# Second pair's attention: where in its step VectorE divides a finished block of rows

## The chip, the cores and the metric

One core of a Trainium2 chip runs the whole program. The metric is device time in microseconds (us) of that core, as the median of separate executions. The profile is one further execution, seen by the hardware profiler.

Engines by the profile's short names: PE is TensorE (matrix products, and transposes as products with the identity), PEld its weight loads, DVE is VectorE, ACT is ScalarE, POOL is GpSimd, SP is SyncE.

## The reference, cut to what matters

Two blocks of two layers each. The change lies in the second block, in the attention part of each of its two layers ("the second pair"). All is float32, with 512 positions and 64 numbers per head. Each layer has three kinds of attention, side by side:

```
a:  6 heads, scores q.k + bias, restricted by a mask (dilated windows), softmax, times v
b:  4 heads, two softmaxes per head:  a = softmax(s1) - lam * softmax(s2);  o = a @ v
    o_b = rms_norm(o) * subln_g * (1 - lam_init)
c:  6 heads of width 96, causal softmax(q.k * scale) @ v
heads = concatenate(o_a, o_b, o_c);  h = layer_norm(ALPHA * x + heads @ w_o)
```

A softmax is kept as unnormalised exponentials until after the product with v. The block of 128 rows that comes out is then divided by its sums. That division is what the change moves.

## The kernel before, in words

The attention of a layer is cut into 80 *units*: one head, one softmax, one block of 128 query rows `i`, and 128, 256, 384 or 512 keys. A unit of kind b comes as two units next to each other (first and second softmax), all others are single. `UNITS` (line 705) is their order. Units 0 to 7 are done early, among projections. The rest go through a software pipeline of steps `st` = 8 to 83, and every engine's program is a loop over the same steps, written out by hand in this order:

- PE (lines 2352 to 2370): `score(st)`, the product q.k of unit `st` into one of three PSUM banks; then, when it is due, `mix(g)`, the products with v of a whole group `g` of finished units; then the transposes of unit `st - 4` (line 2367); then, at five steps, `turn_chunk` (line 2325), the transposes of finished heads.
- ACT (lines 1595 to 1616): copy the transposed unit out of PSUM (line 1602), then `exp2(st)` (lines 1563 and 1566).
- DVE (lines 3066 to 3088): `rows_out2` for a group whose mix is done, then `scored(st)` (line 2986: adds mask or bias to the score and takes the row minimum, from PSUM to SBUF), then `pair(st - 2)` if unit `st - 2` is the second of two (lines 2994 to 2996: joins the two softmaxes of a b unit), then `sub_norm` (two pieces of the norm of the b heads, steps 71 and 72), then the low part `g_lo` of a turned chunk (line 2530).
- POOL (line 942, `two_keys`): makes a head's keys in high and low parts when the last score of an earlier head is done (lines 944 and 947). Its program is no loop over steps.

What ties the engines together: `score(st)` on PE waits until DVE has done `scored(st - 3)`, whose bank it takes. `scored(st)` waits for `score(st)` and for a free SBUF buffer out of five. `exp2(st)` waits for `scored(st)`. `pair(i)` waits for `exp2(i)`, and PE's transposes of unit `i`, four steps after its score, wait for `exp2(i)` or, for a b unit, for `pair(i)`.

`rows_out2` is called with the rank of a turned unit and does something only for the last unit of a group. There are 13 groups: group 0 holds four b blocks; each later group holds the four row blocks of one a or c head, and up to two b blocks more, which are called *singles* in the code. For a group it issues a reciprocal for each single (line 3053), waits for `mix(g)`, takes the reciprocal of four sums (line 3056; for group 0 it is line 3050, ahead of the wait), multiplies 128x256 numbers (line 3057), and then one 128x64 multiply per single (line 3062). Its result is needed by `mix(g + 2)`, which takes the same PSUM bank, and by `turn_chunk`. It acts at these steps (worked out from lines 676 to 771):

```
group      0   1   2   3   4   5   6   7   8   9  10  11
step      15  23  29  37  43  51  57  63  70  74  78  82
singles    0   2   1   2   1   2   1   1   2   0   0   0
steps of the loop with a pair() behind scored(): 15 20 25 30 35 40 44 49 54 59 64
turn_chunk at steps 31 45 59 72 80 (and low part g_lo two steps later)
```

Group 12 is divided after the loop.

Of the kernel before, what the change touches and what calls it, by code (L numbers as in the profile page):

```python
# [262 lines left out]
def _program(nc, I, out, seen):  # L263
    ctx = ExitStack()
    with ctx:
# [444 lines left out]
        def probs_of(i):  # L710

            return strips[:, B_HEADS + EARLY_AT[i], :] if i < EARLY else sc2[(i - EARLY) % N_B]
# [5 lines left out]
        def turns(step):  # L718
            i = step - (N_B - 1)
            return UNITS[i]["rank"] if 0 <= i < len(UNITS) else None  # L720
# [132 lines left out]
        def _(sp):  # L853
            for half in range(2):
                t = 2 * half
                sp.dma_start(res[:, t:t + 2, :], I["x"][0, t * P:(t + 2) * P, :].rearrange("(t p) d -> p t d", p=P)).then_inc(s_x_landed[half].sem, 16)
            for n, (what, _) in enumerate(stream):
                if what == Q0:
                    sp.dma_start(raw_q0[:], I["tiles"][n, :, :]).then_inc(s_q0_landed.sem, 16)
# [1655 lines left out]
        def _(dve):  # L2515
            V = nc.vector

            def step(ins):

                ins.then_inc(s_dve_step.sem, s_dve_step.nth("latest"))  # L2520
                dve.wait_ge(s_dve_step.sem, s_dve_step.count)

            def inverse(key, a, n):

                dve.wait_ge(s_root.sem, s_root.at(key))
                step(V.reciprocal(rstd[:, a:a + n], rstd[:, a:a + n]))

            def lo_part(dst, src, hi, key, wait_key):
                dve.wait_ge(s_hi.sem, s_hi.at(wait_key))
                V.tensor_tensor(dst, src, hi.bitcast(F32), ALU.subtract).then_inc(s_lo.sem, s_lo.nth(key))  # L2530
# [407 lines left out]
            for l in range(DEPTH):  # L2938
# [42 lines left out]
                def scored(i):  # L2981

                    u = UNITS[i]
                    n = u["n"]
                    dve.wait_ge(s_scores.sem, s_scores.at((y, i)))
                    V.tensor_tensor_reduce(probs_of(i)[:, 0:n], ps[:, S_BANKS[i % N_S], 0:n], u["mask"], 1.0, 3.0e38, ALU.add, ALU.min,  # L2986
                                           small[:, 0, i % 8:i % 8 + 1]).then_inc(s_scored.sem, s_scored.nth((y, i)))

                def pair(i):

                    u = UNITS[i]
                    n, ratio = u["n"], small[:, 2, i % 8:i % 8 + 1]
                    dve.wait_ge(s_probs.sem, s_probs.at((y, i)))
                    step(V.reciprocal(ratio, small[:, 1, i % 8:i % 8 + 1]))
                    step(V.tensor_scalar(ratio, ratio, sums[:, u["sum"]:u["sum"] + 1], lam[:, 4:5], ALU.mult, ALU.mult))
                    V.scalar_tensor_tensor(probs_of(i)[:, 0:n], probs_of(i)[:, 0:n], ratio, probs_of(i - 1)[:, 0:n],
                                           ALU.mult, ALU.add).then_inc(s_paired.sem, s_paired.nth((y, i)))
# [21 lines left out]
                def sub_norm(st):  # L3019

                    o = ao[:, :, 384:640].rearrange("p t (h d) -> p t h d", d=HD)
                    sq = sq_b[:].rearrange("p (t h) d -> p t h d", t=XT)
                    if st == B_DONE + 1:
                        dve.wait_ge(s_o_out.sem, s_o_out.at((y, max(group_of[last_of["b", h]] for h in range(B_HEADS)))))
                        step(V.tensor_tensor(sq, o, o, ALU.mult))
                    if st == B_DONE + 2:
                        step(V.tensor_reduce(ssq[:, 0:16], sq_b[:], AX_X, ALU.add))
                        V.tensor_scalar(ssq[:, 0:16], ssq[:, 0:16], 1.0 / HD, 1e-5, ALU.mult, ALU.add).then_inc(s_var.sem, s_var.nth((y, "sub")))
                    if st == STEPS:
                        inverse((y, "sub"), 0, 16)  # L3030
                        step(V.tensor_scalar(rstd[:, 0:16], rstd[:, 0:16], lam_c[:, 1:2], None, ALU.mult))
                        r = rstd[:, 0:16].rearrange("p (t h) -> p t h", t=XT).unsqueeze(3).broadcast_to((P, XT, B_HEADS, HD))
                        step(V.tensor_tensor(o, o, r, ALU.mult))
                        g = subln[:].unsqueeze(1).unsqueeze(1).broadcast_to((P, XT, B_HEADS, HD))
                        V.tensor_tensor(o, o, g, ALU.mult).then_inc(s_sub.sem, s_sub.nth(y))

                def rows_out2(r):

                    g = group_of[r]
                    if r != GROUPS[g][-1]:  # L3040
                        return
                    b = OUT_BANKS[g % 2]
                    singles = [] if g == 0 else [q for q in GROUPS[g] if UNITS[RANKS[q]]["kind"] == "b"]
                    u = [UNITS[RANKS[q]] for q in GROUPS[g] if q not in singles][0]
                    w = HD if g == 0 else VW
                    rows = ps[:, b, 0:XT * w].rearrange("p (i d) -> p i d", d=w)
                    s0 = u["sum"] - u["i"]
                    totals = recips[:, s0:s0 + XT].unsqueeze(2)
                    if g == 0:
                        step(V.reciprocal(totals, sums[:, s0:s0 + XT].unsqueeze(2)))  # L3050
                    for q in singles:
                        x = UNITS[RANKS[q]]
                        V.reciprocal(recips[:, x["sum"]:x["sum"] + 1], sums[:, x["sum"]:x["sum"] + 1]).then_inc(s_b_recip.sem, s_b_recip.nth((y, q)))
                    dve.wait_ge(s_mixed.sem, s_mixed.at((y, g)))
                    if g > 0:
                        step(V.reciprocal(totals, rows[:, :, HD:VW]))
                    m = V.tensor_tensor(ao[:, :, u["col"]:u["col"] + HD], rows[:, :, 0:HD], totals.broadcast_to((P, XT, HD)), ALU.mult)
                    for q in singles:
                        m.then_inc(s_rows_part.sem, s_rows_part.nth((y, q)))
                        x = UNITS[RANKS[q]]  # L3060
                        dve.wait_ge(s_b_recip.sem, s_b_recip.at((y, q)))
                        m = V.tensor_scalar(ao[:, x["i"], x["col"]:x["col"] + HD], ps[:, b, MIXED[q][1]:MIXED[q][1] + HD],
                                            recips[:, x["sum"]:x["sum"] + 1], None, ALU.mult)
                    m.then_inc(s_o_out.sem, s_o_out.nth((y, g)))

                for st in range(EARLY, STEPS):
                    if st - 2 == EARLY + 1:
                        pair(st - 2)
                    if turns(st) is not None and turns(st) >= 3:
                        rows_out2(turns(st) - 3)  # L3070
                    if st < len(UNITS):
                        u = UNITS[st]
                        if st >= EARLY + N_B and UNITS[st - N_B]["first"]:
                            dve.wait_ge(s_paired.sem, s_paired.at((y, st - N_B + 1)))
                        elif st >= EARLY + N_B:
                            dve.wait_ge(s_turned.sem, s_turned.at((y, UNITS[st - N_B]["rank"])))
                        if u["kind"] == "c":
                            dve.wait_ge(s_causal.sem, s_causal.at(y))
                        if u["kind"] == "a":
                            dve.wait_ge(s_strips.sem, s_strips.at(y))  # L3080
                        scored(st)
                    if EARLY + 1 < st - 2 < len(UNITS) and UNITS[st - 2]["second"]:
                        pair(st - 2)
                    sub_norm(st)
                    if st - 2 in turn_at:
                        k = turn_at[st - 2]
                        dve.wait_ge(s_kr_all.sem, s_kr_all.at((y, C_HEADS - 1)))
                        lo_part(g_lo[:, CHUNKS.index(k), :], ps[:, TURNED["chunk", k], :], g_hi[:, CHUNKS.index(k), :], (y, "m", k), (y, "m", k))
# [238 lines left out]
```

## Time and profile before

| what | value |
|---|---|
| median of 3 runs | 1830.11 us (1830.06 to 1830.66) |
| the profiled execution's own time | 1828.74 us |
| its span in the trace | 1826.9 us |
| PE busy | 1779.0 us, 97% of the span |
| PEld / DVE / ACT / POOL busy | 1585.0 / 1196.8 / 912.8 / 777.8 us |
| chain that ended last | PE 85%, DVE 8%, ACT 4%, issue 2%, POOL 1%, DMA 1% |
| the two attention stages (loop over steps) | about 744 to 824 us and 1342 to 1422 us |

A busy share is taken over the whole span, so it says little about one stage: inside the two attention stages the engines share the work in another way than outside. The granted clock of PE is printed as 9 tenths or more in all 40 slices.

### The profile page before, as it was taken

To read this page: it belongs to the slowest core of one execution; us is meant where nothing else is said; L and a number is where in the kernel's file an instruction comes from. 1 tells how busy PE (TensorE), PEld (TensorE's weight loads), DVE (VectorE), ACT (ScalarE), POOL (GpSimd) and SP (SyncE) were. 2 spreads that over 40 slices of the span, in tenths; PEclk is the share of its full clock that TensorE was granted. 3 is DMA by queue.
4 is the path that set the end of the run, shared out by engine and by line. 5 is a ranking of instruction groups with operands and counts; after the bars stand their busy time and mean duration, and the time that the engine had idled before them with its cause. 6 is when DMAs were issued, how large, how long until landed. Compare 5 with 4: busy or idle time off the path is not lost.

```text
span 1826.9 us, 33474 instructions
## 1 busy us (share of the span) xinstructions
PE 1779.0 (97%) x13078; PEld 1585.0 (87%) x13078; DVE 1196.8 (66%) x2313; ACT 912.8 (50%) x1789; POOL 777.8 (43%) x601
## 2 busy tenths in 40 slices
PE   9999999999999999989999999999998999999997
PEld 7898888878898888678999998888877899999886
DVE  5797465269455353785999984256368589998533
ACT  4242276484366474883545443227488255444323
POOL 2544262255553454344443436544424354343652
PEclk9999999999999999999999999999999999999999
DMA  8444141123221232103232323222310323323321
GB/s 337 168 173 167 24 116 60 69 70 139 104 48 55 88 102 107 42 2 139 93 111 98 116 93 126 100 88 92 117 42 2 138 72 114 116 93 116 116 93 46
DMA packets 37032, 182.40 MB, mean 100 GB/s; under 512 B 8288, under 2 KB 9184, under 8 KB 18956
## 3 DMA queue, kind: packets, MB, share of 16 engines
q1 hardware_dynamic: 30664, 168.89, 26.5%
q10 hardware_dynamic: 6212, 11.36, 2.0%
q8 instruction: 106, 1.74, 0.4%
q14 instruction: 50, 0.41, 0.1%
HBM read 178.10 MB, written 5.41 MB: 100 GB/s over the span
## 4 chain that ended last, share of the span: by engine, by line
PE 85%; DVE 8%; ACT 4%; issue 2%; POOL 1%; DMA 1%; DVEq 0%; SPq 0%; ACTq 0%
PE ps L1718 17%; PE ps L1720 17%; PE ps L1719 17%; PE ps L2441 7%; PE ps L2443 7%; PE ps L2442 7%; PE ps L1798 2%; PE ps L1812 2%; PE ps L2346 2%; PE ps L2252 2%; PE ps L1779 1%; PE ps L2367 1%; DVE sc L2986 1%; POOL w_lo L927 1%; ACT pt L1184 1%
## 5 line engine op out<-in xcount | busy, mean ns | idle before, releaser
L927 POOL TENSOR_TENSOR w_lo<-raw,w_hi 128x512 fp32r<-128x512 f32 (+1 forms) x343 | 477.9, 1426 | 616.1 <-ACT w_hi L1057 615.9
L1057 ACT ACTIVATE w_hi<-raw 128x1024 fp32r<-128x1024 f32 (+3 forms) x174 | 170.9, 1026 | 225.8 <-PE ps L1720 208.8
L1033 POOL TENSOR_TENSOR w_lo<-raw,w_hi 128x512 fp32r<-128x512 f32 x80 | 112.7, 1408 | 222.9 <-ACT w_hi L1122 222.7
L1718 PE MATMUL ps<-h_hi,w_lo 128*128 128x512 f32 (+1 forms) x496 | 177.2, 357 | 3.7 <-DVE h_lo L2530 3.6
L1719 PE MATMUL ps<-h_lo,w_hi 128*128 128x512 f32 (+1 forms) x496 | 174.5, 352 | 0.0
L1720 PE MATMUL ps<-h_hi,w_hi 128*128 128x512 f32 (+1 forms) x496 | 174.5, 352 | 0.0
L1718 PE MATMUL ps<-w_hi,hid_lo 128*128 128x512 f32 x352 | 137.1, 390 | 0.0
L1719 PE MATMUL ps<-w_lo,hid_hi 128*128 128x512 f32 x352 | 137.0, 389 | 0.0
L1720 PE MATMUL ps<-w_hi,hid_hi 128*128 128x512 f32 x352 | 136.9, 389 | 0.0
L2530 DVE TENSOR_TENSOR hid_lo<-hid,hid_hi 128x512 fp32r<-128x512 f32 x44 | 65.4, 1529 | 102.1 <-ACT hid_hi L1158 102.1
L1718 PE MATMUL ps<-w_hi,g_lo 128*128 128x512 f32 (+3 forms) x320 | 114.1, 356 | 1.5 <-POOL w_lo L927 1.5
L1720 PE MATMUL ps<-w_hi,g_hi 128*128 128x512 f32 (+3 forms) x320 | 112.1, 350 | 0.0
L1719 PE MATMUL ps<-w_lo,g_hi 128*128 128x512 f32 (+3 forms) x320 | 111.8, 349 | 0.0
L1718 PEld LDWEIGHTS ps<-h_hi,w_lo 128*128 128x128 f32 x496 | 93.8, 189 | 18.6 <-issue 5.5
L1720 PEld LDWEIGHTS ps<-h_hi,w_hi 128*128 128x128 f32 x496 | 93.7, 189 | 12.9
L1719 PEld LDWEIGHTS ps<-h_lo,w_hi 128*128 128x128 f32 x496 | 93.8, 189 | 11.7
L2592 DVE SCALAR_TENSOR_TENSOR acc<-raw,cond,acc 128x512 f32<-128x512 f32 x112 | 98.9, 953 | 0.8 <-DMA raw<-in_tiles 0.7
L1122 ACT ACTIVATE ext_hi<-ps 128x512 fp32r<-128x512 f32 x80 | 47.8, 598 | 95.1 <-DVE ps L3163 69.6
L2441 PE MATMUL ps<-T_hi,w_lo 128*128 128x256 f32 x320 | 90.7, 283 | 0.0
L2441 PE MATMUL ps<-G_hi,w_lo 128*128 128x256 f32 x320 | 90.6, 283 | 0.0
L2442 PE MATMUL ps<-G_lo,w_hi 128*128 128x256 f32 x320 | 90.6, 283 | 0.0
L2443 PE MATMUL ps<-G_hi,w_hi 128*128 128x256 f32 x320 | 90.6, 283 | 0.0
(392 smaller groups left out, 5446.0 us busy)
## 6 DMA issues: line engine op xcount, KB each, us to landing
raw<-in_tiles SPq DMA_DIRECT2D x139, 1024.0 KB, 4.8
strips<-bias_rows ACTq DMA_DIRECT2D x18, 256.0 KB, 4.0
raw<-in_tiles SPq DMA_DIRECT2D x4, 832.0 KB, 4.2
bias_rows<-bias_row SPq DMA_DIRECT2D x10, 320.0 KB, 9.9
raw<-in_tiles SPq DMA_DIRECT2D x4, 768.0 KB, 5.1
res<-in_x SPq DMA_DIRECT2D x2, 1024.0 KB, 6.4
ln<-in_ln_g ACTq DMA_DIRECT2D x4, 512.0 KB, 5.0
ln<-in_ln_b ACTq DMA_DIRECT2D x4, 512.0 KB, 7.6
```

What stands on the lines that cost most here:

```text
L927: pool.tensor_tensor(w_lo[:, i % SPLIT, a:e], raw_of(what)[:, a:e], w_hi[:, i % SPLIT, a:e].bitcast(F32), ALU.subtract).then_inc(s_tile_lo ...
L1033: pool.tensor_tensor(lo, quad_of(what[0], j, name), hi.bitcast(F32), ALU.subtract).then_inc(s_pool_piece.sem, s_pool_piece.nth(((what[0], ...
L1057: act.activation(w_hi[:, i % SPLIT, a:b], raw_of(what)[:, a:b], ACT.Copy).then_inc(s_tile_hi.sem, s_tile_hi.nth((what, n)))
L1122: act.activation(piece_of(y, j, name)[0], src, ACT.Copy).then_inc(s_piece_hi.sem, s_piece_hi.nth((what, name)))
L1718: pe.matmul(o, lhs[1], rhs[0], start=first, stop=False)
L1719: pe.matmul(o, lhs[0], rhs[1], start=False, stop=False)
L1720: return pe.matmul(o, lhs[0], rhs[0], start=False, stop=last)
L2441: pe.matmul(o, lhs[1], rhs[0], start=starts and k == 0, stop=False, skip_group_check=True)
L2442: pe.matmul(o, lhs[0], rhs[1], start=False, stop=False, skip_group_check=True)
L2443: m = pe.matmul(o, lhs[0], rhs[0], start=False, stop=ends and k == 3, skip_group_check=True)
L2530: V.tensor_tensor(dst, src, hi.bitcast(F32), ALU.subtract).then_inc(s_lo.sem, s_lo.nth(key))
L2592: V.scalar_tensor_tensor(to[:], w, by, to[:], ALU.mult, ALU.add).then_inc(s_weigh.sem, s_weigh.nth((what, k, h)))
```

## The change

In each step of the loop the call of `rows_out2` moves from ahead of `scored(st)` to behind `pair(st - 2)`, still ahead of `sub_norm` and of `g_lo`. No instruction is added or taken away; only the order on DVE changes.

```diff
                 for st in range(EARLY, STEPS):
                     if st - 2 == EARLY + 1:
                         pair(st - 2)
-                    if turns(st) is not None and turns(st) >= 3:
-                        rows_out2(turns(st) - 3)
                     if st < len(UNITS):
                         u = UNITS[st]
                         ...
                         scored(st)
                     if EARLY + 1 < st - 2 < len(UNITS) and UNITS[st - 2]["second"]:
                         pair(st - 2)
+                    if turns(st) is not None and turns(st) >= 3:
+                        rows_out2(turns(st) - 3)
                     sub_norm(st)
                     if st - 2 in turn_at:
                         k = turn_at[st - 2]
```

## Rows read from the trace of the kernel before

**Rows 1.** Busy time by stretch, the two attention stages: us, busy us (instructions), clock, DMA.
```profile
742.00:823.00 81.00, 71.73 (x941) 58.19 (x941) 62.99 (x238) 67.55 (x174) 33.18 (x35) 1.00 0.07 21
1345.00:1426.00 81.00, 71.89 (x948) 58.52 (x947) 63.04 (x236) 65.01 (x168) 31.88 (x32) 1.00 0.12 34
```

**Rows 2.** Waits, 742 to 830 us: engine, waiting line, releaser: us, times, longest.
```profile
PE ps L2367 <- DVE sc L2996: 6.8, 8, 1.5
...
DVE recips L3056 <- PE ps L2346: 5.7, 5, 2.0
```

**Rows 3.** Timeline, step 23 (group 1): start, us, instruction, [idle before <-releaser].
```profile
758.51 0.22 DVE L3053 RECIPROCAL recips<-sums 128x1 f32<-128x1 f32 x2
...
758.83 0.36 PE L2252 MATMUL ps<-bk,bq 128*128 128x256 f32 x1
...
759.14 1.02 PE L2252 MATMUL ps<-kc,qc 96*128 96x512 f32 x2
...
759.59 0.41 DVE L2986 CUSTOM_DVE_ANT_0 sc<-ps,strips 128x256 f32<-128x256 f32 x1
...
760.34 0.69 DVE L2986 CUSTOM_DVE_ANT_0 sc<-ps,strips_g 128x512 f32<-128x512 f32 x1 [0.33 <-PE ps L2252]
```

**Rows 4.** Timeline, step 43 (group 4), from its first instruction to the score behind it.
```profile
780.15 0.16 DVE L3053 RECIPROCAL recips<-sums 128x1 f32<-128x1 f32 x1
...
780.96 0.41 DVE L2986 CUSTOM_DVE_ANT_0 sc<-ps,strips_g 128x256 f32<-128x256 f32 x1
```

**Rows 5.** Timeline behind step 15 (group 0): masked score 16, PE's score 19.
```profile
753.57 0.69 DVE L2986 CUSTOM_DVE_ANT_0 sc<-ps,strips_g 128x512 f32<-128x512 f32 x1
...
754.31 0.30 PEld L2252 LDWEIGHTS ps<-kc,qc 96*128 96x128 f32 x2
```

**Rows 6.** Timeline, steps 29 and 30 (group 2).
```profile
765.75 0.42 DVE L2986 CUSTOM_DVE_ANT_0 sc<-ps,strips_g 128x256 f32<-128x256 f32 x1 [0.32 <-PE ps L2367]
...
766.72 0.69 DVE L2986 CUSTOM_DVE_ANT_0 sc<-ps,strips_g 128x512 f32<-128x512 f32 x1 [0.54 <-PE ps L2252]
```

**Rows 7.** Timeline, step 37 (group 3), and PE's score 40.
```profile
775.06 0.22 DVE L3053 RECIPROCAL recips<-sums 128x1 f32<-128x1 f32 x2
...
776.11 0.55 DVE L2986 CUSTOM_DVE_ANT_0 sc<-ps,strips 128x384 f32<-128x384 f32 x1
776.59 0.55 DVE L2986 CUSTOM_DVE_ANT_0 sc<-ps,strips 128x384 f32<-128x384 f32 x1
...
776.72 0.91 PE L2252 MATMUL ps<-kc,qc 96*128 96x384 f32 x2 [0.82 <-DVE small L2986]
```

**Rows 8.** Timeline, steps 51 to 58 (groups 5 and 6).
```profile
791.43 0.45 PE L2248 MATMUL ps<-free_hi,qa 128*128 128x384 f32 x1 [0.39 <-DVE small L2986]
...
794.71 0.42 PE L2252 MATMUL ps<-bk,bq 128*128 128x384 f32 x1
...
795.97 0.69 DVE L2986 CUSTOM_DVE_ANT_0 sc<-ps,strips 128x512 f32<-128x512 f32 x1
```

**Rows 9.** Timeline, pairs of steps 44 and 64, with POOL's low key parts beside them.
```profile
782.16 2.70 POOL L947 TENSOR_TENSOR free_lo<-ka,free_hi 64x512 fp32r<-64x512 f32 x2
...
782.92 0.79 DVE L2996 SCALAR_TENSOR_TENSOR sc<-sc,small,sc 128x256 f32<-128x256 f32 x1
...
802.43 2.69 POOL L947 TENSOR_TENSOR free_lo<-ka,free_hi 64x512 fp32r<-64x512 f32 x2
...
802.87 1.10 DVE L2996 SCALAR_TENSOR_TENSOR sc<-sc,small,sc 128x256 f32<-128x256 f32 x1
```

**Rows 10.** Timeline, steps 70 to 76 (group 8).
```profile
808.18 0.34 PE L2249 MATMUL ps<-free_lo,qa 128*128 128x384 f32 x1
...
808.90 0.55 DVE L2986 CUSTOM_DVE_ANT_0 sc<-ps,strips 128x384 f32<-128x384 f32 x1
...
812.99 0.29 DVE L2986 CUSTOM_DVE_ANT_0 sc<-ps,strips 128x128 f32<-128x128 f32 x1
...
813.34 0.50 PE L2248 MATMUL ps<-free_hi,qa 128*128 128x512 f32 x1
```

## The prediction

> **What bounds the kernel now.** I read the busy time by stretch first. In both attention stages no engine is full: of 81 us PE is busy 71.7, ACT 65 to 68, DVE 63.0 [rows 1]. PE, which is nearly always busy elsewhere, has about 9 us of gaps here, and they are all that the change can reach. The two stages agree to 0.2 us in PE and DVE, so I work out one and double it. Next the table of waits of the first stage [rows 2]. PE's transposes wait 6.8 us in 8 waits for DVE's joined pairs. DVE waits 5.7 us in 5 waits for mixes before it can divide a block. So the stage is a ring of PE, DVE and ACT in which each waits for another in turn, and what an edit is worth depends on who is late where. That is read from the timeline, step by step. A delay of PE here is a delay of the end: behind the stage PE has its own work nearly without a break (97% busy over the whole span), and all that DVE, ACT and POOL do there is timed by PE.
>
> **What the change moves.** The work is the same; 12 divisions per stage come later within their step. Their length is the distance from their first instruction to the score behind them: 759.59 - 758.51 = 1.08 us with two singles [rows 3], 780.96 - 780.15 = 0.81 with one [rows 4]; with none I estimate 0.81 - (1.08 - 0.81) = 0.54. No DMA, no instruction of another engine and no wait is added. The division stands ahead of a pair in the same step at step 15 alone; elsewhere only `scored` changes place with it, and the next pair has it in front of it as before, only nearer. So in 11 of 12 steps the question is: is DVE idle just behind a mix or just behind the score? PE issues `score(st)` behind the mix and the transposes of the step before. A division that starts when the mix is done fills the time in which DVE would wait for that score. Behind the score this cover is gone.
>
> Now each block. A masked score of 384 columns holds DVE 776.59 - 776.11 = 0.48, its 0.55 less 0.07 of overlap [rows 7]; one of 256, 0.41 long, by the same overlap 0.34. For "when is a score ready for DVE" I take the end of PE's product plus 0.18 us: score 24 ends at 759.14 + 1.02 = 760.16, and DVE, idle for it, starts at 760.34 [rows 3].
>
> *Block 0, step 15: +0.5.* The division is behind score 15 and pair 13, where DVE goes on without idle time to masked score 16 at 753.57. This moves to 754.1. PE loads the weights of score 19, which needs score 16's bank, at 754.31, right behind the end of score 16 at 754.26 [rows 5]. Slack 0.05, so PE loses 0.5. Ends: 0 (later slack takes it up) and 0.54.
>
> *Block 1, step 23: +0.4.* Score 23 is ready at 758.83 + 0.36 + 0.18 = 759.37, so it starts 0.22 earlier than now, takes 0.34 to the next instruction, and the division ends at 759.37 + 0.34 + 1.08 = 760.79. Score 24 starts now at 760.34, after 0.33 idle [rows 3]. So a good 0.4 later, and pair 23 with it, for which PE waits (one of the 8 waits [rows 2]). Ends 0 and 0.45.
>
> *Block 2, step 29: +0.2.* Now DVE waits for the mix, divides, waits 0.32 for score 29 and 0.54 for score 30. Behind score 29: 765.75 + 0.34 + 0.81 = 766.90, against 766.72. Pair 28 comes 0.2 later [rows 6], and PE, which waits for it, as well (another of the 8 [rows 2]). Ends 0 and 0.2.
>
> *Block 3, step 37: -0.5.* Here the edit does what it says. Score 37 starts at 775.06 instead of 776.11, and PE's score 40, which waits 0.82 for its bank, no longer does [rows 7]. What is late next is masked score 38, which still starts at 775.06 + 0.48 + 1.08 = 776.6 and ends at 777.2; PE wants its bank for score 41 1.1 us behind score 40, at 777.0. So 0.82 shrinks to about 0.5, which I take: ends 0.8 and 0.4.
>
> *Blocks 4 and 7, steps 43 and 63: 0.* In both DVE reaches the next pair later, by about 0.15 and 0.45 by the same arithmetic. But the two pairs, equal in shape, take 0.79 and 1.10 us, and end at 783.71 and 803.97, each 0.2 us behind POOL's first low key part beside it (782.16 + 1.35 = 783.51 and 802.43 + 1.35 = 803.78) [rows 9]. They end with POOL however early they start, within these delays. POOL itself is timed by PE's score. Ends 0, and 0.15 + 0.45 = 0.6 if the pair isn't held.
>
> The Trainium skill ("SBUF — State Buffer", Who interferes with whom) says that a DVE instruction with two SBUF inputs and a GpSimd instruction that reads SBUF exclude each other, the second to issue blocking until the first is done. The trace agrees, with the two durations just given. Without it the sum below would be 2.3 a stage and not 1.7.
>
> *Blocks 5 and 6, steps 51 and 57: +0.2 together.* At 51 masked score 51 comes 1.05 earlier, and PE's wait of 0.39 for a bank goes. At 57, with PE 0.39 ahead, score 57 is ready at 794.71 + 0.42 - 0.39 + 0.18 = 794.92, the division ends at 794.92 + 0.48 + 0.81 = 796.21, and masked score 58 starts there and not at 795.97 [rows 8]. From there DVE goes on nearly without a break to pair 57, for which PE waits, so the gain is eaten and 0.2 is lost. Ends -0.4 and +0.2.
>
> *Block 8, step 70: +0.9.* The clearest case. DVE waits for mix 8, divides in the time that PE needs for score 70, and starts it at 808.90. Behind the change it starts at 808.18 + 0.34 + 0.18 = 808.7, and the division, with the singles' reciprocals that now run while DVE waits, ends at 808.7 + 0.48 + 1.08 = 810.26. Masked score 71 started at 808.90 + 0.48 = 809.38, so it comes 0.9 later. Behind it DVE has the squares of the b heads, score 72, the sums and score 73, nearly without idle time. Masked score 73 ends at 813.28, and PE starts score 76, which needs that bank, at 813.34 [rows 10]. There is no slack, so PE loses 0.9. Ends 0.5 and 0.9.
>
> *Blocks 9 to 11: 0.* DVE is behind PE's mixes there and idle between; the two low parts behind them start with ACT's high part. Ends 0 and 0.2.
>
> **Sum.** 0.5 + 0.4 + 0.2 - 0.5 + 0 + 0.2 + 0.9 = 1.7 us a stage, 3.4 for two. The profiled execution took 1828.74 us; it becomes 1832.1. It lay 1.4 below the median of the runs, 1830.11, and I carry that over: 1833.5.
>
> **Rivals.**
> *Bank release wins (not slower).* One mechanism: masked scores come earlier, so that PE gets its score banks earlier, at steps 40 and 54, and the delays behind are taken up by DVE's idle time. Price 0.8 + 0.4 = 1.2 a stage: 1830.1 - 2.4 = 1827.7. It decides if PE wants masked scores 19 and 76 more than 0.5 and 0.9 us behind their present end. For it: both waits are there. Against: the slack that I read is 0.05 and 0.06.
> *It does all it could.* If PE were spared the divisions of blocks 3, 5, 6, 7 and 8, behind which DVE goes on at once, that is 1.05 + 1.05 + 0.8 + 0.8 + 0.9 = 4.6 a stage, or 1820.9. PE's 6.8 us of waits for pairs would pay for it, but only one pair is passed.
> *Nothing changes.* Work is conserved, gains and losses cancel: 1830.1.
> *Slower by more.* The pairs of blocks 4 and 7 are not held by POOL (+0.6), and the bank at step 41 takes back block 3 (+0.5): 2.8 a stage, 1835.7.
> *A later division holds up who needs its result.* The turned chunks at steps 45 and 72 follow it by two steps. By the times above division 8 ends at 810.3, and PE turns chunk 0 about then; 0.2 us, inside the 0.9. No case of its own.
>
> **How the numbers follow.** A measurement of this kernel can tell about 0.2%, 3.7 us, from no change: the bounds are 1826.4 and 1833.8. Forecast 0.50, its own range 1831.6 to 1835.4, and nearly half of it (0.24) lies above the bound. Slower by more 0.18, all above. Nothing changes 0.13. Bank release wins 0.13, of which 0.02 below the lower bound. All it could 0.06, below. So slower 0.42, same 0.50, faster 0.08. The range goes from the bank release's 1827.7, with 0.3 for the spread of runs, to the slower rival's 1835.7 with as much: 1827.4 to 1836.0; it leaves out about 0.15.
>
> **What would show it.** PE's waits for pairs should grow from 6.8 to about 7.5 us a stage; its 0.8 us wait for a bank at step 40 should go and a shorter one at 41 come; a new wait of nearly 0.9 should stand before PE's score 76, and one of 0.5 before score 19. DVE's 5.7 us of waiting for mixes should shrink to the last blocks' share, and its waits for PE's scores grow. The pairs of steps 44 and 64 should keep their distance to POOL's low parts. The prediction is wrong if PE's gaps in the stage shrink, if score 76 doesn't wait, or if the stage's length, from unit 8's masked score to the first projection behind it, moves by less than 1 us.

## The result and the profile after

The kernel after takes 1837.07 us, the median of 5 runs (1836.22 to 1839.43), against 1830.11 of the kernel before (1829.5 to 1830.66, 5 runs): a ratio of 1.0039, 95% interval 1.0027 to 1.0051. It is 7.0 us slower. I had forecast 1833.5 in a range of 1827.4 to 1836.0. The sign of the likely case was right; the time lies above the range. One timed execution of the kernel code_shift, below, took 4503.09 us against 1832.37 to 1834.97 in its ten others, and is left out of the ratio given there.

The profiled execution has a span of 1835.3 us and 1837.07 as its own time. Where did it lose? I compare the masked scores one by one. A masked score's delay is its start after, counted from the start of unit 8's, less the same in the kernel before. The sum of the forecast stands beside it.

| masked score | blocks in front of it | forecast, sum | first stage | second stage |
|---|---|---|---|---|
| 16 | 0 | 0.5 | 0.54 | 0.54 |
| 24 | 0, 1 | 0.9 | 0.95 | 0.94 |
| 30 | to 2 | 1.1 | 1.13 | 1.11 |
| 41 | to 3 | 0.6 | 0.62 | 0.59 |
| 59 | to 6 | 0.8 | 0.82 | 0.80 |
| 65 | to 7 | 0.8 | **2.12** | 0.75 |
| 71 | to 8 | 1.7 | **4.52** | 1.63 |
| 79 | to 10 | 1.7 | 4.91 | 2.00 |

4.91 + 2.00 = 6.9 us: these two stages are as good as the whole difference of the medians. (PE itself is 4.8 and 1.9 late when it starts the first product behind the stage, L1718.) (The two profiled executions differ by 8.3; the first stage of after begins 1.55 later, in work that is the same in both, and in the other kernels below from 0.3 earlier to 2.8 later, whatever was changed in them.) Up to step 62 the sum holds in both stages, and in the second it holds to the end, but for 0.3. The first stage alone has 2.9 more, and all of it arises between masked scores 63 and 71.

Waits of the changed kernel, first stage, 742 to 834 us (engine, waiting line, releaser: us, times, longest). They answer to [rows 2]:

```profile
PE ps L2367 <- DVE sc L2996: 8.1, 8, 2.8
...
DVE recips L3056 <- PE ps L2346: 3.4, 2, 1.9
...
PE ps L2252 <- DVE small L2986: 0.5, 2, 0.3
...
PE ps L2248 <- DVE small L2986: 0.2, 1, 0.2
```

The same view of the second stage, 1345 to 1440 us:

```profile
PE ps L2367 <- DVE sc L2996: 6.9, 8, 1.6
```

DVE's waits for mixes fell from 5.7 to 3.4 us, as the change intends. PE's waits for pairs stayed (6.9) in the second stage and grew to 8.1 in the first. One wait alone makes that: 2.8 us instead of 1.5. It is the pair of step 64. The timeline of both stages around it (start, us, instruction, [idle before <-releaser]), against [rows 9]:

```profile
802.98 0.28 PE L2249 MATMUL ps<-free_lo,qa 128*128 128x256 f32 x1
...
803.79 0.42 DVE L2986 CUSTOM_DVE_ANT_0 sc<-ps,strips 128x256 f32<-128x256 f32 x1 [0.76 <-PE ps L2367]
...
804.75 2.60 POOL L947 TENSOR_TENSOR free_lo<-ka,free_hi 64x512 fp32r<-64x512 f32 x2
...
806.05 1.58 DVE L2996 SCALAR_TENSOR_TENSOR sc<-sc,small,sc 128x256 f32<-128x256 f32 x1
...
807.69 0.44 PE L2367 MATMUL ps<-ident,sc 128*128 128x128 f32 x2 [2.79 <-DVE sc L2996]
...
1405.67 0.28 PE L2249 MATMUL ps<-free_lo,qa 128*128 128x256 f32 x1
...
1406.13 0.42 DVE L2986 CUSTOM_DVE_ANT_0 sc<-ps,strips 128x256 f32<-128x256 f32 x1 [0.42 <-PE ps L2367]
...
1407.45 2.69 POOL L947 TENSOR_TENSOR free_lo<-ka,free_hi 64x512 fp32r<-64x512 f32 x2
...
1408.40 0.60 DVE L2996 SCALAR_TENSOR_TENSOR sc<-sc,small,sc 128x256 f32<-128x256 f32 x1
1409.05 0.44 PE L2367 MATMUL ps<-ident,sc 128*128 128x128 f32 x2 [1.62 <-DVE sc L2996]
```

POOL's two low parts of a key stand in one row, 2.60 us x2. Views that begin and end between the two show each by itself, first stage:

```profile
804.75 1.26 POOL L947 TENSOR_TENSOR free_lo<-ka,free_hi 64x512 fp32r<-64x512 f32 x1
...
806.09 1.26 POOL L947 TENSOR_TENSOR free_lo<-ka,free_hi 64x512 fp32r<-64x512 f32 x1
```

So the first part ends 1.26 behind its start, and the second starts 0.08 later. In the second stage the pair starts 0.95 behind POOL and ends at 1409.00, 0.3 behind the end of the first part (1407.45 + 1.26 = 1408.71), as I had forecast. In the first stage it starts 1.30 behind POOL, in the 0.08 us between the two parts, and takes 1.58 us. It ends at 807.63, 0.28 behind the end of the *second* part (807.35). The difference begins at masked score 63: its product ends at 803.26 and DVE starts it 0.53 later, in the second stage 0.18 later.

Busy time of five microseconds behind it (us, PE busy, PEld, DVE, ACT, POOL, granted clock, DMA share, GB/s):

```profile
807.00:808.00 1.00, 0.31 (x3) 0.31 (x4) 1.00 (x4) 0.12 (x1) 0.35 (x1) 1.00 0.00 0
808.00:809.00 1.00, 1.00 (x8) 0.84 (x7) 0.76 (x4) 1.00 (x4) 0.50 (x1) 0.81 0.00 0
809.00:810.00 1.00, 1.00 (x6) 0.89 (x5) 0.52 (x1) 0.72 (x3) 0.86 (x3) 0.50 0.03 8
...
811.00:812.00 1.00, 1.00 (x25) 1.00 (x24) 0.00 (x0) 0.40 (x1) 0.92 (x2) 0.50 0.00 0
812.00:813.00 1.00, 1.00 (x36) 0.96 (x32) 0.00 (x0) 0.00 (x0) 0.48 (x1) 0.99 0.00 0
```

The granted clock is 0.50 (1.2 GHz) from 808.6, some 0.9 us behind the wait, for 3.4 us, until 812; elsewhere in both stages it is 1.00 (2.4 GHz). PE is busy all through, only slower. So the theory has two parts: 1.35 us because the pair meets POOL's second low part, and about 1.5 because the clock falls behind PE's 2.8 us without work.

### The profile page after: what moved, and what is told of

Read it like the earlier page. It is cut to its first block, busy times and chain, and to the rows that moved or that the text cites. A ratio compares the mean times of both kernels' runs of the same rounds, so it can differ in the third digit from the quotient of the medians.

```text
span 1835.3 us, 33474 instructions
## 1 busy us (share of the span) xinstructions
PE 1784.9 (97%) x13078; PEld 1587.3 (86%) x13078; DVE 1196.7 (65%) x2313; ACT 912.4 (50%) x1789; POOL 777.2 (42%) x601
## 4 chain that ended last, share of the span: by engine, by line
PE 86%; DVE 8%; ACT 4%; issue 2%; POOL 1%; DVEq 0%; ACTq 0%; POOLq 0%
PE ps L1718 17%; PE ps L1720 17%; PE ps L1719 17%; PE ps L2441 7%; PE ps L2443 7%; PE ps L2442 7%; PE ps L1798 2%; PE ps L2346 2%; PE ps L1812 2%; PE ps L2367 2%; PE ps L1779 1%; PE ps L2252 1%; DVE sc L2986 1%; PE ps L1829 1%; POOL w_lo L927 1%
## 5 line engine op out<-in xcount | busy, mean ns | idle before, releaser
L1718 PE MATMUL ps<-h_hi,w_lo 128*128 128x512 f32 (+1 forms) x496 | 177.2, 357 | 4.3 <-DVE h_lo L2530 3.7
L1718 PE MATMUL ps<-w_hi,hid_lo 128*128 128x512 f32 x352 | 137.1, 390 | 0.0
L1718 PE MATMUL ps<-w_hi,g_lo 128*128 128x512 f32 (+3 forms) x320 | 114.1, 356 | 1.5 <-POOL w_lo L927 1.3
L1718 PEld LDWEIGHTS ps<-h_hi,w_lo 128*128 128x128 f32 x496 | 93.8, 189 | 19.3 <-issue 5.6
```

Source lines behind the costliest of these rows:

```text
L1718: pe.matmul(o, lhs[1], rhs[0], start=first, stop=False)
```

## The experiments

Each was timed beside the kernel before on the same chip: 1829.47, 1829.71 and 1830.22 us in the three groups.

### Does block 7 do it?

**block7_ahead.** The kernel after, with block 7 alone left ahead of its score. Against the kernel before it is this edit, with BEHIND all blocks but 7; four kernels below have the same edit with another set.

```
-                    if turns(st) is not None and turns(st) >= 3:
+                    if turns(st) is not None and turns(st) >= 3 and group_of[turns(st) - 3] not in BEHIND:
                         rows_out2(turns(st) - 3)
...
                         pair(st - 2)
+                    if turns(st) is not None and turns(st) >= 3 and group_of[turns(st) - 3] in BEHIND:
+                        rows_out2(turns(st) - 3)
                     sub_norm(st)
```

> The changed kernel, but the division of group 7 (step 63) stays ahead of the masked score, in both stages. Theory H: in the first stage the pair of step 64 starts about 0.8 us earlier, within POOL's first low part, is held by that one alone, and there is no fall of the clock: 1837.1 - 1.35 - 1.5 = 1834.2. Rival R, by which block 7 costs its own delay of 0.45 us a stage and nothing more: 1836.2.

1833.2 us (1832.33 to 1834.27), ratio 1.0011 to 1.0029, 1.0 below the 1834.2 of the theory. The pair starts 0.44 behind POOL, as in the kernel before:

```profile
802.96 2.69 POOL L947 TENSOR_TENSOR free_lo<-ka,free_hi 64x512 fp32r<-64x512 f32 x2
803.40 1.10 DVE L2996 SCALAR_TENSOR_TENSOR sc<-sc,small,sc 128x256 f32<-128x256 f32 x1
804.56 0.44 PE L2367 MATMUL ps<-ident,sc 128*128 128x128 f32 x2 [1.52 <-DVE sc L2996]
```

Masked score 79 is 2.05 and 2.06 late in the two stages: the first now behaves as the second.

**only7.** The other way round: the kernel before, with block 7 alone moved (BEHIND is {7}).

> The kernel before with only block 7 (step 63) divided behind its score. Theory (the step that failed): whether the pair of step 64 costs nothing or much hangs on whether it still starts beside POOL's first low key part. In the kernel before it starts 0.66 us behind the first low part's start; it moves by about 0.45, so it should start about 0.3 us before that part ends and be held by it alone: pair ended by the first low part, PE's wait for it about 1.5 us, granted clock 1.00 behind it, masked score 65 later by 0 to 0.3 us, whole time equal to the kernel before within 0.5 us. Rival (moving block 7 costs by itself what it cost in the changed kernel): masked score 65 later by 1.2 us or more in the first stage, whole time longer by 1.5 to 3 us. A start of masked score 63 delayed by 0.3 us and more would tip it to the rival's side in that stage.

1831.98 us (1829.83 to 1834.38), ratio 1.0001 to 1.0019. The profiled execution is the slowest of the eleven. In it masked score 65 is 1.34 late in the first stage and 0.01 in the second; masked score 71 is 2.88 and 0.01 late. The condition that I had named for the rival's side came true: masked score 63 starts with 0.78 us of idle time before it in the first stage, 0.41 in the second.

```profile
804.27 0.42 DVE L2986 CUSTOM_DVE_ANT_0 sc<-ps,strips 128x256 f32<-128x256 f32 x1 [0.78 <-PE ps L2367]
...
805.22 2.60 POOL L947 TENSOR_TENSOR free_lo<-ka,free_hi 64x512 fp32r<-64x512 f32 x2
...
806.53 1.57 DVE L2996 SCALAR_TENSOR_TENSOR sc<-sc,small,sc 128x256 f32<-128x256 f32 x1
...
808.16 0.44 PE L2367 MATMUL ps<-ident,sc 128*128 128x128 f32 x2 [2.78 <-DVE sc L2996]
```

The pair again starts between the two parts, and takes 1.57 us. So the second stage came out as the theory had it, and the first as the rival. In this execution block 7 alone reproduces all that I had missed at its place, the fall of the clock with it. Its median is 2.3 above the kernel before, between what the two stages would give with and without the event (2.9 and 0), so some of its executions may be without it; only this one was profiled.

**code_shift.** Why is masked score 63 late in the first stage only? DVE's program is the same in both. One guess was that its instructions arrive late there. The kernel after with 24 small stores in DVE's program ahead of the stage's loop, which shifts where the later instructions lie:

```
+                for _ in range(24):
+                    step(V.memset(lam[:, 7:8], 0.0))
                 dve.wait_ge(s_strips_b.sem, s_strips_b.at(y))
```

> The changed kernel, with 24 tiny memsets on DVE in its idle time ahead of the loop, in both layers; nothing else moves. In the first stage masked score 63 starts 0.36 us later than its product allows, in the second it does not, and a transfer of code by the instruction queues lies at that moment. Theory C: DVE's code arrives late there, and only this delay carries the pair over the edge of POOL's first low part. Then another place in the code meets the transfer, masked score 63 starts on time, the pair is held by the first low part alone: about 1834.3. Rival: the delay has to do with the program's data and order: 1837.1, and masked score 63 starts 0.36 late as before.

1833.86 us, ratio 1.0012 to 1.0031 (1834.3 expected). Masked score 63 is on time in the first stage, and the pair is held by the first part:

```profile
802.35 0.42 DVE L2986 CUSTOM_DVE_ANT_0 sc<-ps,strips 128x256 f32<-128x256 f32 x1 [0.41 <-PE ps L2367]
...
803.67 2.69 POOL L947 TENSOR_TENSOR free_lo<-ka,free_hi 64x512 fp32r<-64x512 f32 x2
...
804.62 0.60 DVE L2996 SCALAR_TENSOR_TENSOR sc<-sc,small,sc 128x256 f32<-128x256 f32 x1
```

Masked score 79 is 2.10 and 2.05 late. So the position of the instructions decides, or goes with what decides. Masked score 63 is late by the same 0.36 in the first stages of keys4_late and pe_filled too, and in no second stage. That it is the arrival of the instructions I can't call shown: the profile has transfers of instructions near that spot in all of these kernels, and in only7 the 16 KB one comes 1.5 us behind the late start.

### The pair against POOL's two parts

Three kernels with nothing moved: the kernel before with 4, 8 or 14 small stores in front of DVE's pair in step 64.

```
+                    if st == 64:
+                        for _ in range(4):            # 8; 14
+                            step(V.memset(lam[:, 7:8], 0.0))
                     if EARLY + 1 < st - 2 < len(UNITS) and UNITS[st - 2]["second"]:
                         pair(st - 2)
```

**push4.**

> The kernel before, nothing moved; in step 64 four small stores (0.124 us each) stand in front of DVE's pair, so it starts 0.5 us later, about as far as block 7 pushes it. It then starts at about 0.3 us before POOL's first low key part ends. Theory (a staircase): the pair is held until that part ends and no longer, so it ends where it did; masked score 65 0 later, each stage 0 to 0.1 longer, whole time as the kernel before within 0.4 us. Rival (a late pair costs its lateness): +0.5 a stage, +1.0 in the whole.

**push8.**

> As with four stores, but eight: the pair starts 1.0 us later than in the kernel before, a little behind the end of POOL's first low key part. Theory: it is now held to the end of the second low part: it ends 1.3 us later than in the kernel before, PE waits 2.8 us for it in both stages and masked score 65 is 1.3 later. If a wait of this length lets the granted clock of TensorE fall, 1.5 us more come with it: +2.9 a stage, +5.7 in the whole; with a fall in one stage only +4.2, in none +2.7. Rival (a late pair costs its lateness): +1.0 a stage, +2.0 in the whole, and nothing of the clock.

**push14.**

> As with eight stores, but fourteen: the pair starts 1.7 us later than in the kernel before, still before POOL's second low key part ends. Theory: six stores more cost nothing more, since the pair ends with the same part: PE waits 2.8 us, masked score 65 1.3 later, the whole as with eight stores within 0.5 us. Rival: +1.7 a stage, +3.5 in the whole without the clock, and 0.75 a stage above the kernel with eight.

| stores | pair starts later by | masked score 65 later by (stage 1, 2) | masked score 79 later by | median, against before |
|---|---|---|---|---|
| 4 | 0.5 | -0.02, -0.02 | -0.02, -0.03 | 1829.79, -0.4 |
| 8 | 1.0 | 1.31, 1.34 | 2.83, 2.88 | 1836.07, +5.9 |
| 14 | 1.8 | 1.31, 1.32 | 2.83, 2.87 | 1835.26, +5.0 |

The ratios are 0.9989 to 1.0007, 1.0020 to 1.0045 and 1.0019 to 1.0038. It is a staircase: half a microsecond costs nothing, another half costs 2.9 us a stage, and 0.75 more nothing again. The rival, that a late pair costs its lateness, would have had +1.0, +2.0 and +3.5. First stages of the three kernels, one after the other:

```profile
803.84 2.68 POOL L947 TENSOR_TENSOR free_lo<-ka,free_hi 64x512 fp32r<-64x512 f32 x2
804.81 0.57 DVE L2996 SCALAR_TENSOR_TENSOR sc<-sc,small,sc 128x256 f32<-128x256 f32 x1
```

```profile
802.70 2.59 POOL L947 TENSOR_TENSOR free_lo<-ka,free_hi 64x512 fp32r<-64x512 f32 x2
804.17 1.39 DVE L2996 SCALAR_TENSOR_TENSOR sc<-sc,small,sc 128x256 f32<-128x256 f32 x1
...
805.62 0.44 PE L2367 MATMUL ps<-ident,sc 128*128 128x128 f32 x2 [2.83 <-DVE sc L2996]
```

```profile
804.73 2.59 POOL L947 TENSOR_TENSOR free_lo<-ka,free_hi 64x512 fp32r<-64x512 f32 x2
806.95 0.65 DVE L2996 SCALAR_TENSOR_TENSOR sc<-sc,small,sc 128x256 f32<-128x256 f32 x1
```

The pair ends 0.28 behind a low part each time: behind the first (803.84 + 1.26 = 805.10) with four stores, behind the second (802.70 + 2.59 = 805.29, 804.73 + 2.59 = 807.32) with eight and with fourteen. PE waits for it 1.5, 2.8 and 2.85 us.

### Does the clock cost the rest?

**push8_fed.** As with eight stores, and PE does 20 products of the identity while it would wait for the pair.

```
+                        if step == 66:
+                            pe.wait_ge(*emptied[b])
+                            for _ in range(20):
+                                pe.transpose(ps[:, b, 0:P], ident[:], ident[:])
                         if UNITS[i]["second"]:
                             pe.wait_ge(s_paired.sem, s_paired.at((y, i)))
```

> As with eight stores, and PE does 20 products of the identity with itself (0.12 us each) into the bank that it is about to use, before it waits for the pair of step 64; they hold nothing up, since the pair comes later still. They replace 2.4 of the 2.8 us in which PE would stand idle. Theory: the time lost to the clock is due to PE's idleness; the granted clock stays 1.00 behind the pair in both stages, masked score 65 is 1.3 later, and the stage ends 1.3 to 1.4 longer: +2.7 in the whole, and up to 3 us less than with eight stores alone. Rival (what is lost behind the late pair is DVE's or ACT's, or the clock falls for another reason): the same time as with eight stores.

1832.68 us (1831.45 to 1836.04), ratio 1.0006 to 1.0023: +2.5 us, and 3.4 less than the same kernel without the products (2.7 and 3 expected). Masked score 65 is 1.35 late in the first stage, and nothing is added to it up to masked score 79 (1.34). In the second the pair costs as much (1.35), but 1.55 us had been lost there already ahead of masked score 15, by a fall of the clock that the last section tells of, and masked score 79 is 2.95 late. The microseconds behind the pair without the products and with them (columns as above; the pair ends at 805.56 and 807.62):

```profile
807.00:808.00 1.00, 1.00 (x8) 0.88 (x8) 0.70 (x2) 0.97 (x3) 0.86 (x3) 0.52 0.03 8
808.00:809.00 1.00, 1.00 (x20) 1.00 (x22) 0.43 (x4) 0.89 (x2) 1.00 (x1) 0.50 0.00 0
```

```profile
809.00:810.00 1.00, 1.00 (x21) 0.93 (x21) 0.78 (x3) 1.00 (x4) 0.86 (x3) 1.00 0.03 8
810.00:811.00 1.00, 1.00 (x42) 1.00 (x40) 0.27 (x4) 0.81 (x2) 1.00 (x1) 1.00 0.00 0
```

So DVE's late pair is worth 1.35 us a stage and the clock 1.5 on top, and behind the pair the products, which do no useful work, give the 1.5 back.

**pe_filled.** An earlier try at the same: the kernel after with 12 such products.

> The changed kernel, with 12 products of the identity with itself on PE in step 66, ahead of its wait for the pair of step 64, into the bank that the transposes behind them overwrite. They take about 0.7 to 1.3 us of a wait of 2.8 us in the first stage and 1.6 in the second, so they delay nothing. Theory H: the clock's fall comes from the idle time, so it stays at 1.00 and 1.5 us are saved: 1835.6; the pair is still held. If the fall has another cause: 1837.1 and a clock of one half for 4 us as before.

1835.47 us, ratio 1.0023 to 1.0046. The number is near the 1835.6 expected, but by luck: the profiled execution tells nothing on this question. There the pair of the first stage starts 1.30 us behind POOL, between its two low parts, as in the kernel after, and this time it isn't held. It takes 0.49 us, and the second low part, which starts 0.05 behind it (a view that begins behind the first, as above), takes 1.57 instead of 1.26:

```profile
807.18 0.49 DVE L3000 SCALAR_TENSOR_TENSOR sc<-sc,small,sc 128x256 f32<-128x256 f32 x1
...
807.23 1.57 POOL L947 TENSOR_TENSOR free_lo<-ka,free_hi 64x512 fp32r<-64x512 f32 x1
```

So at the edge of the staircase, between the two parts, either can be the one that is held: in the kernel after and in only7 POOL's second part starts 0.04 and 0.03 behind the pair, and the pair is held. There was no long wait to fill, and PE waited 0.39 us for the pair behind the products. 1.54 us were lost elsewhere in the first stage, between masked scores 8 and 15, as the last section tells. That is why push8_fed starts from a kernel in which the second part holds the pair in both stages.

**keys4_late.** The other side of the collision: the kernel after, and POOL's keys of head 4 wait for masked score 67 and not 63, so that they come behind the pair of step 64.

```
-  pool.wait_ge(s_scores.sem, s_scores.at((y, SCORED_LAST["c", 3 + h] if h < 3 else SCORED_LAST["a", h - 3])))
+  pool.wait_ge(s_scores.sem, s_scores.at((y, {4: 67}.get(h, SCORED_LAST["c", 3 + h] if h < 3 else SCORED_LAST["a", h - 3]))))
```

> The changed kernel (1837.1 us), but POOL makes the keys of head a4 after score 67 and not after score 63, so that it reads no SBUF tensor while the pair of step 64 runs. Theory H: in the first stage that pair (1.58 us) starts just behind the end of POOL's first low part, is held through the second, PE idles 2.8 us, its clock falls to one half, and products run slow for 4 us. Then the pair takes 0.5 us in both stages, PE's longest wait in the first stage falls to about 1.6, the clock stays at 1.00, and the time is 1837.1 - 1.1 - 1.5 - 0.1 = 1834.4. Rival R: the first stage's extra delay comes from the order on DVE itself, whatever POOL does: 1836.5 to 1837.1.

1836.17 us (1835.1 to 1836.99), ratio 1.0022 to 1.0047: little better than the kernel after, where I had expected 1834.4. The pair is free now, but POOL's work has moved onto another instruction of DVE:

```profile
805.91 0.48 DVE L2996 SCALAR_TENSOR_TENSOR sc<-sc,small,sc 128x256 f32<-128x256 f32 x1
...
806.45 0.44 PE L2367 MATMUL ps<-ident,sc 128*128 128x128 f32 x2 [1.70 <-DVE sc L2996]
...
812.67 3.49 POOL L947 TENSOR_TENSOR free_lo<-ka,free_hi 64x512 fp32r<-64x512 f32 x2
...
812.99 2.04 DVE L3025 TENSOR_TENSOR sq_b<-ao 128x1024 f32<-128x1024 f32 x1
```

Pair 0.48 us long, PE's wait for it 1.70, masked score 65 1.00 late: the collision is gone, and so is the fall of the clock. But the squares of the b heads take 2.04 us, where the kernel after has 1.22 for them. Masked score 79 is 3.07 late in the first stage (4.91 in the kernel after) and 2.75 in the second (2.00). My expectation had the first effect and not the second.

### The terms one by one

**only8.** The kernel before with block 8 alone moved (BEHIND is {8}).

> The kernel before with only block 8 (step 70) divided behind its score. Theory: this is the largest single loss of the change that hangs on nothing else: PE waits 0.9 us before its score 76 in each stage, and the stage ends 0.9 later. Whole time +1.8 us on the kernel before. Rival (the loss at step 70 is only what reached it from the earlier blocks): 0 to +0.4 us.

1831.98 us (1830.24 to 1833.39), ratio 1.0003 to 1.0021. Masked score 71 is 0.86 and 0.88 late, 79 is 0.85 and 0.86. The largest term stands by itself.

**gains35.** The kernel before with blocks 3 and 5 alone moved (BEHIND is {3, 5}).

> The kernel before with only blocks 3 and 5 (steps 37 and 51) divided behind their scores, the two places where PE's wait for a score bank went away and nothing else was late. Theory: -0.5 us at block 3 and -0.4 at block 5 in each stage as long as the pairs behind them are not held by POOL; -1 to -1.8 us in the whole. Rival (any gain is taken back at the pairs beside POOL's low key parts and in PE's other waits): 0. A second rival: the pair of step 64 comes to lie against another of POOL's parts and the stage loses 1 us or more.

1828.05 us (1827.42 to 1829.91), ratio 0.9982 to 1.0000. Masked score 37 comes 1.05 earlier and 51 1.56 (1.05 more than 50), masked score 41 0.49 and 0.51, and from 57 to 79 all come 0.88 and 0.89 earlier. The two gains reach the end.

**best.** In gains35 the pairs of steps 44 and 49 are held by POOL. Here the keys of heads 0, 1 and 2 wait for one masked score more (36, 44 and 50, in place of 35, 43 and 49), in the same line as in keys4_late.

> As the kernel with only blocks 3 and 5 moved, and beside it POOL's keys of heads 0, 1 and 2 are held back by one masked score each (36, 44 and 50 in place of 35, 43 and 49), so that the pairs of steps 35, 44 and 49 are issued ahead of POOL's low key parts or beside its first cast. Theory: the pair of step 44 takes 0.5 us and not 0.79, those of 35 and 49 are not held either, 0.3 to 0.6 us less a stage: -1.6 to -3 us in the whole against the kernel before. Rival (POOL, being later, holds other instructions of DVE that read two inputs from SBUF, as it did when head 4 was held back): no better than only blocks 3 and 5, or worse by up to 1.5 us.

1827.26 us (1826.78 to 1827.97), ratio 0.9978 to 0.9996. It is the fastest of all (lowest median and lowest range), 2.5 us below the kernel before, and 9.8 below the kernel after by their two medians, which were taken apart. The pairs of steps 44 and 49, first in gains35, then here:

```profile
782.90 2.71 POOL L947 TENSOR_TENSOR free_lo<-ka,free_hi 64x512 fp32r<-64x512 f32 x2
783.67 0.80 DVE L2996 SCALAR_TENSOR_TENSOR sc<-sc,small,sc 128x256 f32<-128x256 f32 x1
...
788.43 2.96 POOL L947 TENSOR_TENSOR free_lo<-ka,free_hi 64x512 fp32r<-64x512 f32 x2
788.65 1.60 DVE L2996 SCALAR_TENSOR_TENSOR sc<-sc,small,sc 128x512 f32<-128x512 f32 x1
```

```profile
783.30 0.48 DVE L2996 SCALAR_TENSOR_TENSOR sc<-sc,small,sc 128x256 f32<-128x256 f32 x1
783.50 2.77 POOL L947 TENSOR_TENSOR free_lo<-ka,free_hi 64x512 fp32r<-64x512 f32 x2
...
787.97 0.75 DVE L2996 SCALAR_TENSOR_TENSOR sc<-sc,small,sc 128x512 f32<-128x512 f32 x1
```

The first pair goes from 0.80 us to 0.48 and the second from 1.60 to 0.75. That of step 35 goes from 1.23 to 0.35, and no masked score behind it comes earlier by that. The pair of step 59 now lies beside a low part and takes 0.90 instead of 0.62, which gives 0.29 of the gain back. Masked score 79 comes 1.35 and 1.36 us earlier than in the kernel before. The interval against the kernel before ends just below 1; against gains35 the two ranges overlap, and the 0.8 us between their medians agree with the 0.47 a stage that the traces show.

## Why the prediction was wrong, by its own steps

**Blocks 0 to 6: right.** +0.54, +0.41, +0.18, -0.51, 0 for block 4, and +0.2 for blocks 5 and 6, each within 0.1 of its term in both stages.

**Block 7, step 63: here it failed**, in the first stage alone. "They end with POOL however early they start, within these delays." I had put the case of no hold at 0.6 as the upper end. The hold itself was right, and the sentence I took from the Trainium skill ("SBUF — State Buffer", Who interferes with whom) holds in every row above, in pe_filled with POOL as the one that is held. But I used it for one instruction of POOL only. POOL has two low parts in a row, 0.08 us apart. A pair that comes behind the end of the first isn't free; in all but that one case it waits for the second as well. The numbers for that stood in [rows 9]: POOL's row is 2.69 us long for two, and the pair started 0.44 behind it. I halved the row, which leaves 1.35 - 0.44 = 0.91; the first part by itself is 1.26 us long, which leaves 0.82. I estimated a delay of 0.45, and it measures 0.5 (pair 0.95 behind POOL in the second stage). 0.31 of the room was left, and a late start of 0.36 us of masked score 63, in the first stage alone, took more than that. The price behind that edge is 1.35 us, and then the clock falls behind PE's wait of 2.8 us, 1.5 more. Neither stood in my bounds: 2.9 against an upper end of 0.6. With it the sum is 1.7 + 1.7 + 2.9 = 6.3, or 1836.4 us.

**Block 8: right in size, half right in its way.** +0.88 in the second stage, +0.86 alone. I had all of it at PE's score 76, and put the wait of chunk 0 for division 8 at 0.2 inside the same 0.9. In only8 PE's turn of chunk 0 comes 0.4 later, and the other half comes at score 76, where PE stands 0.2 and its weight load 0.45. A forecast wait of "nearly 0.9" before score 76 isn't in the waits; the sum is.

**Blocks 9 to 11: +0.3 where I had 0**, upper end 0.2. It is block 10. Up to the mix of step 77 PE is as late as at score 76 (1.61 in the second stage); its turn of a chunk in step 80 is 1.91 late. The loading of its weights waits there for block 10's division, which step 78 now does behind masked score 78. First stage:

```profile
824.28 0.42 PEld L2325 LDWEIGHTS ps<-ident,ao 128*128 128x128 f32 x4 [0.34 <-DVE ao L3057]
```

Masked score 79, with the same division in front of it, is 0.4 later than 78. With 0.3 twice the sum is 6.9, or 1837.0 us, against 1837.07 measured.

**The rivals.** "Slower by more" was the nearest, 1835.7, by mechanisms that did not come about: the bank at step 41 took back no more than the sum allows (PE waits 0.17 there), and the pairs were held. "A later division holds up who needs its result" was called no case of its own and tied to steps 45 and 72; PE's weights now wait 0.2 to 0.55 us for a division at all five turned chunks, and at step 80 that reaches the end. "Bank release wins" decided by slack behind masked scores 19 and 76, and the slack was as short as read: PE now waits 0.32 for score 19. Its two gains are real, as gains35 shows, and they are the part of the change worth keeping.

What would have put it right: to ask of block 7 not only "until when is the pair held" but "what holds it if it comes later", and to take the next instruction of POOL's queue as the upper end.

## What to carry to other kernels

The delay of an instruction that is held by another engine's instruction is hidden only up to the end of that one. If a second of the same kind follows with hardly a gap, the cost of a delay is a staircase, so read its distance to the edge and price the next step, not the delay. A long single wait of TensorE must be priced with the clock behind it, which here doubled it. And a move of many places in one loop should be tried place by place: here two of twelve gained, by their traces, and the rest lost or did nothing.

## What the runs showed of the hardware

The fall of the clock isn't set by the kernel alone. PE waited 2.8 us for the pair of step 64 in six stages of the profiled kernels (the first of after and of only7, both of push8 and of push14), and the granted clock was 0.50 for 3.4 us behind each, at a cost of 1.5 to 1.6 us where it can be read alone. Behind the 1.5 to 1.7 us that it waited in the other stages without added products it stayed 1.00. But another wait, of 1.32 us whose end lies 4.3 us behind the first masked score, is the same in all fourteen profiled kernels. Behind it the clock stayed up in 26 of 28 stages, and fell in two: in the first stage of pe_filled and in the second of push8_fed. In pe_filled (its lines stand four lower than in the kernel before):

```profile
749.79 0.66 PE L2371 MATMUL ps<-ident,sc 128*128 128x128 f32 x4 [1.32 <-DVE sc L3000]
```

and a microsecond behind it (columns as above):

```profile
751.00:752.00 1.00, 1.00 (x19) 0.97 (x20) 0.56 (x2) 0.00 (x0) 0.00 (x0) 0.54 0.08 16
```

Both falls cost 1.54 to 1.55 us, and the clock was 0.50 for the same 3.4 us. Both are in kernels with added products, though some 55 us ahead of those of their stage; why there stays open. Events of this size may be a part of the spread of the timed runs, 2 to 4 us between the lowest and the highest of one kernel; that was not tested.
